# Expert biases of a mixture-of-experts block: loaded as four rows and spread by a VectorE shuffle

## The chip, the cores and the metric

The kernel runs on one core of one Trainium2 chip. The metric is the device time in microseconds (us) of one execution; smaller is better. Three runs of the kernel before took 1596.85, 1597.67 and 1598.76 us.

## What is computed

One residual block over 512 tokens of width 1024 with 16 meta tokens ahead. The first part (a convolution branch, an mLSTM branch and an output projection) isn't touched by the change. The second part is a mixture of experts: a router picks 4 of 32 experts for each token, and each expert computes, for the tokens that chose it,

```
hcat = xb @ w1[e] + b1[e]              # 1024 -> 2048
h_glu, h_lin = split(hcat)             # both clamped at 7.0
act = h_glu * sigmoid(1.702 * h_glu) * (h_lin + 1)
y = act @ w2[e] + b2[e]                # 1024 -> 1024
out = sum over the 4 experts of a token of gate * y
```

All in 32-bit floats. An expert has 8 MB of `w1`, 4 MB of `w2`, 8 KB of `b1` and 4 KB of `b2`.

## The kernel before

The engines each have their own program and meet at semaphores. The first part and the router end with the placing of tokens into slots: each expert has 96 slots (`SLOTS`), cut in three tiles of 32 (`TG = 3`). With the given data one pass over the 32 experts does.

**Weights.** A ring of 12 buffers of 1 MB each holds the weights of an expert: chunks 0 to 7 are `w1` (128 of its rows each), chunks 8 to 11 are `w2`. The SP queue issues all loads in order (`load_block`, `load_chunk`, L484 and L488). Chunk c of expert e is issued when TensorE has used up chunk c of expert e - 1: for c = 0 to 4 one by one through `ring_used`, 5 and 6 the same way at the expert's last tile, 7 with `hid_mm`, and 8 to 11 at the end of the second layer. Behind the last expert's chunks stand the four loads of `y_in`, 2 MB each, which bring back the experts' results in token order for the sums.

**One expert on TensorE (PE).** The hidden layer: for k = 0 to 4 and each tile, four products side by side, one for each group `g` of 32 output partitions (`tile_position=(0, 32 * g)`), of 32 slots by 512 columns (L1619). This layout, in which the 32 partitions of group g hold the 32 slots of a tile and the columns of that group, is why a bias has to stand on 32 partitions at once. After k = 4 come the bias products (below). Then for each tile the k = 5 to 7 (`LATE = 3`), after which the tile is complete (`hid_mm`). The second layer, L1668, follows tile by tile into banks 3 to 5, with the transposes of the next expert's rows (L1606) behind its first tile. Each 32-bit product is two instructions in the trace.

**Biases before.** Ahead of the loop all biases are loaded three times into `bias_rest` (96 partitions of 3 x 1024 values), and VectorE (DVE) subtracts their upper halves (L2077), so that `bias_top` holds three 16-bit parts of each. For each expert, ScalarE (ACT) makes `row_pick`, a matrix that picks that expert's three rows; PE multiplies, four products of 512 columns (L1639) and four of 256 (L1645), into banks 3 and 4; ACT copies them to `bias1` (L1108) and `bias2` (L1110). PE waits for `y_made` ahead of these products, since banks 3 and 4 have held the results of the expert before.

**One expert on the others.** DVE waits for `hid_mm`, adds the bias (L2118), clamps, multiplies, and transposes to `actT` (L2131), tile by tile; then it adds `bias2` to each tile of the second layer as `y_out` (L2144). ACT takes the sigmoid (L1116) and copies the transposed rows to `xT`. GpSimd (POOL) gathers the rows for the expert after next (`xs`, from `u2_rows`) and scatters `y_out` to `y_rows`, both by indirect DMA, through a queue of its own on the same DMA engines.

**Ahead of the loop.** POOL computes `rstd` of each token tile (L610, L611), DVE scales it to `u2` (L1995), and PE, ACT and DVE form logits and choices; POOL writes the token codes to `slot_table` (L717) and reads them back. After the last expert DVE sums: `y_in` times gate (L2187), with the last expert's results added from PE.

## Time and profile before

| | |
|---|---|
| median of three runs | 1597.67 us |
| the profiled execution's own time | 1599.56 us |
| its span, first to last instruction | 1597.8 us |
| outside the span | 1.8 us |
| mean granted clock of TensorE | 0.997 |
| PE busy | 1571.5 us (98%) |
| DVE busy | 649.7 us (41%) |
| POOL busy | 444.7 us (28%) |
| ACT busy | 384.0 us (24%) |
| first hidden product of expert 0 | at 542.06 us |
| moved by DMA | 493.10 MB, of them 384 loads of 1 MB for the ring |

The profile is one execution. Its times are from the start of the span. A matmul's end is modelled and matmuls overlap, so the starts say more than the busy time. In a timeline, a row is a run of like instructions: start, duration, engine, line, operation, output <- inputs, count, and in brackets the idle time ahead of it and what ended it. A landing time is the time from the issue of a transfer to its last part's arrival.

### The profile page before, as it was taken

The numbers are of one execution on the slowest core, as the hardware profiler recorded it, in microseconds if no ns is written. First come the engines' busy times: TensorE is split into PE (matmuls) and PEld (weight loads), VectorE is DVE, ScalarE is ACT, GpSimd is POOL, SyncE is SP. The second block draws the span as 40 slices with busy tenths as digits, with TensorE's granted clock in tenths as the row PEclk, the third lists the DMA queues.
The fourth block names the chain that finished last, engine by engine and source line by source line (L and its number), as shares of the span: only waits on it lengthen the run. The fifth ranks groups of instructions, "written<-read, shape, count | busy, mean of one in ns | idle before, by whom it ended". The sixth has DMA issues, their size and how long they took to land.

```text
span 1597.8 us, 38945 instructions
## 1 busy us (share of the span) xinstructions
PE 1571.5 (98%) x16458; PEld 902.0 (56%) x16458; DVE 649.7 (41%) x1249; ACT 384.0 (24%) x601; POOL 444.7 (28%) x513
## 2 busy tenths in 40 slices
PE   7999999999999999999999999999999999999997
PEld 6998988877889644334433344334433443344334
DVE  4799898016242742224222332233222322232248
ACT  5333134346222311111111121122112111211112
POOL 7334333462433642111211111111211121112114
PEclk9999999999999999999999999999999999999999
DMA  7553242321275699999999999999999999999995
GB/s 217 159 179 112 79 144 95 90 72 51 79 294 224 204 340 406 407 416 414 412 398 410 412 409 398 414 407 408 394 411 407 410 392 404 411 412 400 403 413 236
DMA packets 129781, 493.10 MB, mean 309 GB/s; under 512 B 14379, under 2 KB 72099, under 8 KB 79973
## 3 DMA queue, kind: packets, MB, share of 16 engines
q1 hardware_dynamic: 110932, 464.61, 74.6%
q0 software_dynamic: 9168, 16.78, 3.2%
q10 hardware_dynamic: 9632, 11.03, 2.2%
q8 instruction: 35, 0.57, 0.1%
q14 instruction: 14, 0.11, 0.0%
HBM read 476.32 MB, written 24.87 MB: 314 GB/s over the span
## 4 chain that ended last, share of the span: by engine, by line
PE 95%; POOL 1%; ACT 1%; SPq 1%; DMA 1%; DVE 1%; issue 0%; POOLq 0%; DVEq 0%; ACTq 0%
PE banks L1619 41%; PE banks L1147 27%; PE banks L1668 21%; PE banks L1606 2%; DMA stage<-in_w_in_dram 1%; PE banks L1551 0%; PE banks L1639 0%; SPq L461 0%; PE banks L1506 0%; POOL h_res L787 0%; PE banks L1379 0%; POOL w_lo L624 0%; POOL w_lo L633 0%; POOL small L611 0%; SPq L447 0%
## 5 line engine op out<-in xcount | busy, mean ns | idle before, releaser
L1619 PE MATMUL banks<-w_ring,xT 128*32 128x512 f32 x6144 | 670.9, 592 | 0.1
L1619 PEld LDWEIGHTS banks<-w_ring,xT 128*32 128x32 f32 x6144 | 197.8, 110 | 431.3 <-issue 422.4
L1668 PE MATMUL banks<-w_ring,actT 128*32 128x256 f32 x6144 | 343.9, 380 | 0.0
L1668 PEld LDWEIGHTS banks<-w_ring,actT 128*32 128x32 f32 x6144 | 195.3, 110 | 144.8 <-issue 19.3
L2118 DVE TENSOR_TENSOR hid<-banks,bias 128x512 f32<-128x512 f32 x96 | 63.8, 665 | 475.6 <-PE banks L1619 475.6
L633 POOL TENSOR_TENSOR w_lo<-stage,w_hi 128x2048 fp32r<-128x2048 f32 x38 | 175.3, 4614 | 258.0 <-ACT w_hi L832 258.0
L1147 PE MATMUL banks<-u_hi,w_hi 128*128 128x264 f32 (+1 forms) x528 | 176.8, 335 | 1.5 <-POOL w_lo L624 1.5
L1147 PE MATMUL banks<-u_hi,w_lo 128*128 128x264 f32 (+1 forms) x528 | 175.1, 332 | 0.0
L1147 PE MATMUL banks<-u_lo,w_hi 128*128 128x264 f32 (+1 forms) x528 | 174.7, 331 | 0.0
L706 POOL COPY token_now<-token_of 96x1 int32 x32 | 6.6, 205 | 541.0 <-PE banks L1606 540.9
L1108 ACT ACTIVATE bias<-banks 128x512 f32<-128x512 f32 x32 | 19.1, 598 | 568.4 <-PE banks L1639 568.4
L1809 DVE SCALAR_TENSOR_TENSOR banks<-conv_in,taps,banks 128x512 f32<-128x512 f32 x224 | 151.0, 747 | 0.1
L2144 DVE TENSOR_TENSOR y_out<-banks,bias 128x256 f32<-128x256 f32 x96 | 40.8, 425 | 229.5 <-PE banks L1668 228.3
L1147 PEld LDWEIGHTS banks<-u_hi,w_hi 128*128 128x128 f32 x528 | 99.6, 189 | 11.7 <-POOL w_lo L624 1.7
L1147 PEld LDWEIGHTS banks<-u_lo,w_hi 128*128 128x128 f32 x528 | 99.6, 189 | 10.1
L1147 PEld LDWEIGHTS banks<-u_hi,w_lo 128*128 128x128 f32 x528 | 99.6, 189 | 9.5 <-issue 0.2
L832 ACT ACTIVATE w_hi<-stage 128x2048 fp32r<-128x2048 f32 x40 | 76.4, 1910 | 105.6 <-PE banks L1147 99.0
L695 POOL TENSOR_TENSOR carrier<-carrier 1x1 f32<-1x1 f32 x161 | 33.3, 207 | 240.4 <-DMA y_rows<-y_out,row_now 152.5
L766 POOL DMA_INDIRECT y_rows<-y_out,row_now x93 | 93.5, 1005 | 15.2 <-issue 15.2
L1116 ACT ACTIVATE sig<-hid 128x256 f32<-128x256 f32 x96 | 40.0, 417 | 194.2 <-DVE hid L2119 194.2
L2128 DVE TENSOR_TENSOR act_v<-hid,sig 128x256 f32<-128x256 f32 x96 | 59.8, 623 | 3.5 <-DVE hid L2126 0.3
L1123 ACT ACTIVATE xT<-banks 128x384 f32<-128x384 f32 x64 | 27.9, 488 | 80.0 <-PE banks L1606 80.0
(311 smaller groups left out, 1586.7 us busy)
## 6 DMA issues: line engine op xcount, KB each, us to landing
w_ring<-in_expert_w_dram SPq DMA_DIRECT2D x384, 1024.0 KB, 17.6
stage<-in_w_in_dram SPq DMA_DIRECT2D x20, 1024.0 KB, 5.3
stage<-in_w_in_dram SPq DMA_DIRECT2D x16, 512.0 KB, 5.6
y_rows<-empty_row ACTq DMA_DIRECT2D x8, 1024.0 KB, 4.8
y_in<-y_rows SPq DMA_DIRECT2D x4, 2048.0 KB, 20.8
stage<-in_conv_pw_w_dram SPq DMA_DIRECT2D x4, 1024.0 KB, 5.2
stage<-in_mlstm_out_w_dram SPq DMA_DIRECT2D x4, 1024.0 KB, 5.2
stage<-in_w_out_dram SPq DMA_DIRECT2D x4, 1024.0 KB, 5.5
```

The source lines that it names most:

```text
L633: nc.gpsimd.tensor_tensor(w_lo[:, s], stage[:, s], w_hi[:, s].bitcast(F32), ALU.subtract).then_inc(w_lo_made[s], 1)
L695: nc.gpsimd.tensor_tensor(carrier[:, 1 + i:2 + i], carrier[:, 0:1], carrier[:, 0:1], ALU.add).then_inc(idx_step, 1)
L766: pool.indirect_dma_start(out=y_dram, out_offset=bass.IndirectOffsetOnAxis(ap=row_now[:, t:t + 1], axis=0), in_=y_out[:, t], in_offset=Non ...
L832: nc.scalar.activation(w_hi[:, s], stage[:, s], ACT.Copy).then_inc(w_hi_made[s], 1)
L1116: nc.scalar.activation(sig[:, t], hid[:, t, 0:GRP], ACT.Sigmoid, scale=ALPHA).then_inc(sig_made, 1)
L1147: last = nc.tensor.matmul(dst, l, r, start=(k == 0 and n == 0), stop=(k == KT - 1 and n == 2))
L1619: last = nc.tensor.matmul(banks[32 * g:32 * (g + 1), t].rearrange("p (c j) -> p c j", j=64), xT[:, k, 32 * t:32 * (t + 1)], units, start=k ...
L1668: last = nc.tensor.matmul(banks[32 * g:32 * (g + 1), 3 + t, 0:GRP], actT[:, t, k], w2_ring[k // 2][:, k % 2, GRP * g:GRP * (g + 1)], start ...
L1809: nc.vector.scalar_tensor_tensor(out=to, in0=src, scalar=taps[:, ct, w:w + 1], in1=acc, op0=ALU.mult, op1=ALU.add).then_inc(conv_step, 1)
L2118: own(nc.vector.tensor_tensor(hid[:, t], banks[:, t], bias1.rearrange("p h n -> p (h n)"), ALU.add))
L2128: own(nc.vector.tensor_tensor(act_v[:, t].rearrange("p (c q j) -> p c j q", q=2, j=32), lin.rearrange("p (c j q) -> p c j q", q=2, j=32), ...
L2144: nc.vector.tensor_tensor(y_out[:, t], banks[:, 3 + t, 0:GRP], bias2, ALU.add).then_inc(y_made, 1)
```

## The change

The biases stay in memory and are loaded for each expert as four rows, one for each group g, at partitions 0, 32, 64 and 96 of `bias_row` (zeroed once by POOL; the row for group g holds the 512 hidden and 256 output biases of that group). A VectorE `stream_shuffle` with the mask `[0] * 32` copies the first partition of each 32 over all 32, into `bias`, in 32 bits. The load for the next expert is issued on the SP queue behind its chunk 3, after a wait for the shuffle of the expert before. PE's bias products, ACT's copies and `row_pick`, POOL's `expert_row`, DVE's subtractions, and the threefold load of all biases are gone. PE's wait for `y_made` moves from ahead of the last early products to ahead of the second layer.

```diff
--- before
+++ after
@@ SP, ahead of the loop
-            for m in range(PARTS):
-                sp.dma_start(bias_rest[NE * m:NE * (m + 1), 0:2 * D], expert_b1[0]).then_inc(bias_in, 16)
-                sp.dma_start(bias_rest[NE * m:NE * (m + 1), 2 * D:3 * D], expert_b2[0]).then_inc(bias_in, 16)
+            def load_bias(e):
+                sp.dma_start(bias_row[0:P:32, 0:2 * GRP].rearrange("g (c j) -> g c j", j=64),
+                             expert_b1[0, bass.ds(e, 1)].rearrange("e (c g j) -> (e g) c j", g=CG, j=64)).then_inc(bias_in, 16)
+                sp.dma_start(bias_row[0:P:32, 2 * GRP:3 * GRP],
+                             expert_b2[0, bass.ds(e, 1)].rearrange("e (g n) -> (e g) n", g=CG)).then_inc(bias_in, 16)
+            load_bias(0)
@@ SP, load_block
                     load_chunk(e, c)
+                    if c == 3:
+                        sp.wait_ge(bias_made, n)
+                        load_bias(e)
@@ POOL, ahead of the loop
             pool.wait_ge(mm_done, pair_tick(WO_PAIR + 1, 8))
+            nc.gpsimd.memset(bias_row, 0.0)
...
-            nc.gpsimd.memset(xs, 0.0)
-            for m in range(PARTS):
-                chain(nc.gpsimd.tensor_copy(expert_row[NE * m:NE * (m + 1), 0:NE], ident[NE * m:NE * (m + 1), NE * m:NE * (m + 1)]))
-            nc.gpsimd.tensor_copy(expert_row[:, NE:NE + 1], expert_row[:, 0:1]).then_inc(moe_consts, 1)
+            nc.gpsimd.memset(xs, 0.0).then_inc(moe_consts, 1)
@@ ACT, each expert
-                    act.wait_ge(bias_mm, n * 2 + 1)
-                    nc.scalar.activation(bias1, banks[:, 3].rearrange("p (h n) -> p h n", h=2), ACT.Copy).then_inc(bias_made, 1)
-                    act.wait_ge(bias_mm, n * 2 + 2)
-                    nc.scalar.activation(bias2, banks[:, 4, 0:GRP], ACT.Copy).then_inc(bias_made, 1)
-                    pick_rows(e + 1)
@@ PE, each expert
-                        if k == KT - LATE - 1:
-                            pe.wait_ge(bias_split, PARTS - 1)
-                            pe.wait_ge(y_made, n * TG + 1)
-                            pe.wait_ge(bias_made, n * 3 + 1)
...
-                            for g in range(CG):
-                                last = nc.tensor.matmul(
-                                    banks[32 * g:32 * (g + 1), 3].rearrange("p (c j) -> p c j", j=64), row_pick,
-                                    bias_top[:, 0:2 * D].rearrange("p (c g j) -> p g c j", g=CG, j=64)[:, g],
-                                    start=True, stop=True, tile_position=(0, 32 * g))
-                            last.then_inc(bias_mm, 1)
-                            for g in range(CG):
-                                last = nc.tensor.matmul(banks[32 * g:32 * (g + 1), 4, 0:GRP], row_pick,
-                                                        bias_top[:, 2 * D + GRP * g:2 * D + GRP * (g + 1)],
-                                                        start=True, stop=True, tile_position=(0, 32 * g))
-                            last.then_inc(bias_mm, 1)
@@ PE, second(t)
-                        pe.wait_ge(bias_made, n * 3 + 3)
+                        if t == 0:
+                            pe.wait_ge(y_made, n * TG + 1)
@@ DVE, ahead of the loop
-            dve.wait_ge(bias_in, 16 * 2 * PARTS)
-            for m in range(1, PARTS):
-                rows = slice(0, NE * (PARTS - m))
-                if m > 1:
-                    dve.wait_ge(bias_split, m - 1)
-                nc.vector.tensor_tensor(bias_rest[rows], bias_rest[rows], bias_top[rows], ALU.subtract).then_inc(bias_split, 1)
@@ DVE, each expert (bias1 and bias2 become parts of bias)
-                    dve.wait_ge(bias_made, n * 3 + 2)
+                    dve.wait_ge(y_made, n * TG + 1)
+                    dve.wait_ge(bias_in, n * 32 + 32)
+                    nc.vector.tensor_copy(bias_seen, bias_row[0:1, 0:1])
+                    nc.vector.stream_shuffle(bias, bias_row, [0] * 32).then_inc(bias_made, 1)
+                    dve.wait_ge(bias_made, n + 1)
```

## Rows read from the trace of the kernel before

**Rows 1.** The page: busy us of each engine; DMA busy tenths by slice.

```profile
PE 1571.5 (98%) x16458; PEld 902.0 (56%) x16458; DVE 649.7 (41%) x1249; ACT 384.0 (24%) x601; POOL 444.7 (28%) x513
...
DMA  7553242321275699999999999999999999999995
```

**Rows 2.** Timeline of PE around one expert: start us, us, instruction, count.

```profile
1025.88 13.06 PE L1619 MATMUL banks<-w_ring,xT 128*32 128x512 f32 x120
1038.76 0.41 PE L1639 MATMUL banks<-bias_rest,row_pick 96*32 96x512 bf16 x4
...
1039.11 7.91 PE L1619 MATMUL banks<-w_ring,xT 128*32 128x512 f32 x72
...
1058.13 1.45 PE L1619 MATMUL banks<-w_ring,xT 128*32 128x512 f32 x9
```

**Rows 3.** Ring loads issued from 608 to 1243 us, issue to landing.

```profile
DMA to landing us min/median/max: 12.8/17.6/19.7
```

**Rows 4.** DMA queues, 1012 to 1022 us: packets, MB, share of 16 engines.

```profile
q1 hardware_dynamic: 581, 4.23, 101.6%
```

**Rows 5.** One ring load of a late expert, and its landing.

```profile
L484 SPq DMA_DIRECT2D w_ring<-in_expert_w_dram x1: 333/333/333, 1498.8 to 1498.8; - x1
...
DMA to landing us min/median/max: 22.5/22.5/22.5
```

**Rows 6.** Timeline of PE, 1509.5 to 1536 us.

```profile
1522.90 7.91 PE L1619 MATMUL banks<-w_ring,xT 128*32 128x512 f32 x72
```

**Rows 7.** Timeline of DVE from the last expert on.

```profile
1548.34 1.77 DVE L2177 STREAM_TRANSPOSE selT<-sel_in 128x1536 f32<-128x1536 f32 x1
...
1567.47 3.92 DVE L2187 SCALAR_TENSOR_TENSOR h_res<-y_in,gate_now,h_res 128x1024 f32<-128x1024 f32 x3
...
1574.91 0.42 DVE L2144 TENSOR_TENSOR y_out<-banks,bias 128x256 f32<-128x256 f32 x1 [0.64 <-PE banks L1668]
```

**Rows 8.** Groups by line, DVE: busy us, mean ns, idle before, releaser.

```profile
L2118 DVE TENSOR_TENSOR hid<-banks,bias 128x512 f32<-128x512 f32 x96 | 63.8, 665 | 475.6 <-PE banks L1619 475.6
```

**Rows 9.** DMA queues, 40 to 45 us, while 512 B pieces moved.

```profile
q1 hardware_dynamic: 2064, 1.04, 76.8%
```

**Rows 10.** The page, part 3: the queue of ACT's transfers.

```profile
q10 hardware_dynamic: 9632, 11.03, 2.2%
```

**Rows 11.** DMA issues by line: count, KB each, us to landing.

```profile
y_rows<-empty_row ACTq DMA_DIRECT2D x8, 1024.0 KB, 4.8
...
probs<-head_rows ACTq DMA_DIRECT2D x4, 256.0 KB
inter_bc<-head_rows ACTq DMA_DIRECT2D x4, 256.0 KB, 3.9
...
g_bc<-in_norm_mix_g_dram ACTq DMA_DIRECT2D x1, 512.0 KB, 4.8
...
head_rows<-m_row ACTq DMA_DIRECT2D x1, 8.0 KB
head_rows<-inter_row ACTq DMA_DIRECT2D x1, 8.0 KB
```

**Rows 12.** The first two loads of y_in, issue to landing.

```profile
DMA to landing us min/median/max: 17.1/19.4/21.6
```

**Rows 13.** Timeline ahead of the loop, 526 to 530 us.

```profile
527.55 1.29 DVE L1995 SCALAR_TENSOR_TENSOR u<-h_res,small,gf_bc 128x1024 f32<-128x1024 f32 x1 [1.10 <-POOL small L611]
...
529.04 0.95 POOL L686 MEMSET xs<- 96x1024 f32 x1
...
529.41 0.19 DVE L2015 TENSOR_TENSOR logits<-banks,rb_bc 128x32 f32<-128x32 f32 x1 [0.57 <-PE banks L1569]
```

**Rows 14.** Timeline around the start of the loop.

```profile
541.08 0.96 POOL L717 DMA_INDIRECT slot_table<-code,dest  x1 [0.30 <-issue]
...
542.11 6.72 DVE L2077 TENSOR_TENSOR bias_rest<-bias_rest 64x3072 f32<-64x3072 f32 x2
542.35 3.93 POOL L717 DMA_INDIRECT slot_table<-code,dest  x1 [0.30 <-DVE token_now L2071]
```

24 lines of the change are left out of this document (7 added, 17 removed).

## The prediction, made before the change was run

> **What bounds the kernel now.** I read the page first. TensorE (PE) is busy for 98% of the span, and the busy row of the DMA engines stands at nine tenths in nearly every slice of the second part, at about 410 GB/s [rows 1]. Two resources look full, and a busy share cannot say which one sets the time. So the next view is the timeline of one expert. There PE starts the early products of an expert at 1025.88 us and those of the next at 1058.13: an expert costs 32.25 us, PE never sits idle in it, and the bias products fill the time from the end of a run of 120 products to the start of the next run [rows 2]. PE sets the time, today.
>
> The second question is how far the weights' transfers are from setting it. For that I read the time from issue to landing of the ring's loads. From 608 to 1243 us, some 20 experts, the median stays at 17.6 us and the longest at 19.7 [rows 3]. A transfer that found the engines free would not need that: ten microseconds of pure ring traffic carry 4.23 MB, so 1 MB goes through in 2.48 us, with the queue's packets filling 101.6% of the engines [rows 4]. So about seven loads are always queued. A queue that neither grows nor shrinks over 20 experts is served at just the rate at which it is filled: the engine that lands last needs about 32.25 us for an expert too, and at the end it needs more. In the last experts the load of the eighth chunk, issued at 1498.8, took 22.5 us, against 19.7 before [rows 5], and so landed at 1521.3. PE began the products that need it at 1522.90 [rows 6]. The margin there is 1.6 us. In the middle it was larger: a load issued like it, one period before 1039.11 us [rows 2], was issued at about 1015.0 (1498.8 less 15 periods) and with the longest 19.7 landed 4.4 us ahead.
>
> **What the change takes from PE.** A run of 120 products takes 13.06 us by its row, but its matmuls overlap; starts tell more. From 1025.88 to the first bias product at 1038.76 are 12.88 us, and from there to the next weight product at 1039.11 are 0.35 us [rows 2]. Eight bias products go for each of 32 experts: 32 x 0.35 = 11.2 us. The waits of PE on the bias (`bias_made`, `bias_split`) go as well and cost nothing today, since PE is never idle.
>
> **What it adds on VectorE (DVE).** The shuffle moves 128x768 values. Nearest row: a transpose of 128x1536 in 1.77 us, so half of that, about 0.9 us [rows 7]; it can be no dearer than the whole 1.8 us, which would still be hidden. It stands right after the last `y_out` of the expert before, and DVE then waits for the first `hid_mm`; these waits sum to 475.6 us over 32 experts, some 15 us each [rows 8]. The small copy ahead of it is hidden likewise. In the last expert the selection for the sums stands there too, whose transpose ends at 1550.1, and that expert's late products, whose end DVE waits for, start only at about 1555.2 (1522.90 plus a period) [rows 6, 7]. ScalarE loses three small instructions an expert, off the path. Cost: 0.
>
> **What it adds on SP's queue.** `load_bias(e)` stands behind chunk 3 and waits for the shuffle of the expert before, which is done some 2 us into that expert; chunk 3 is freed at about 10.3 us (four of five runs of 24 products in 12.88 us). Behind the wait stand chunks 4 to 11. It would hold them back only if the bias rows landed over 30 us after their issue (a period of 32.25 less the shuffle and the waits around it). With 20 to 24 us in sight: 0.
>
> **What it adds on the DMA engines.** This is the term that decides. Each expert gets a load of 32 pieces of 256 B (8 KB) and one of 4 pieces of 1 KB, in the same queues as the weights. Price of a piece: while the queue moved 512 B pieces it had 76.8% of 16 engines over 5 us for 2064 packets, 30 ns each [rows 9]. The weights' pieces run at 8192 B in about 310 ns, 26 B per ns [rows 4], so 512 B are 19 ns of bytes and 11 ns of something fixed. Then 256 B are 21 ns, 1 KB is 50 ns; a completion packet is at most the 11. Bounds: bytes alone, 10 and 39 ns; the whole 30 ns for 256 B.
>
> How many engines share it? The trace has transfers of four rows: `head_rows`. The ACT queue moved 9632 packets in all [rows 10]. Its 17 transfers over 128 partitions are y_rows 8 x 1024 packets of 1 KB, probs and inter_bc 8 x 128, g_bc 128: 9344 [rows 11]. The two of four rows are 8 more, which leaves 280 = 17 x 16 + 2 x 4. So a transfer over 128 partitions ends with 16 completions and one of four rows with four: four engines carry it. The bias loads have four rows each. An engine of these four gets 8 x 21 + 50 + 2 x 11 = 240 ns for each expert, 31 times: 7.4 us. By bytes alone it is 8 x 10 + 39 + 22 = 141 ns, 4.4 us; by 30 ns, 312 ns, 9.7 us. Spread over 16 engines, it would be 2 x 21 + 13 + 22 = 77 ns, 2.4 us.
>
> On this the page "DMA: Bandwidth & Descriptors" of the Trainium skill, section "Why a DMA increments its semaphore by 16 and not by 1", says that a transfer runs on the largest number of engines up to 16 that divides the slowest dimension, and on SP's and ACT's queues on the lowest-numbered ones; the count of 280 agrees with the number, and nothing here shows which four. By it, the same four engines would be hit every time; if it failed and 16 shared the load, the sum would be 2.4 us of DMA time in place of 7.4.
>
> **The last stretch.** After the ring come the four `y_in` loads. The first was issued at 1549.42 and landed 17.1 us later, at 1566.5, and DVE's sums over it start at 1567.47: 0.9 us of margin [rows 7, 12]. From there DVE is nearly without a gap to the end; it waited 0.64 us for PE once [rows 7]. So if the transfers end late by x, the end is late by x - 0.9 - 0.6.
>
> **Before the loop.** PE starts the experts at 542. The zeroing of `bias_row` stands on GpSimd (POOL) ahead of the last `rstd`; by the row of 96x1024 in 0.95 us it is 0.7 us. DVE waits for that `rstd` ahead of the last `u2`, which then comes at 528.25 and not 527.55 and ends at 529.5; DVE had 0.57 us idle behind it, and its next step was at 529.41 [rows 13]. Cost: 0.2 us. Against it, the two subtractions of 6.72 us on DVE go; while they ran, an issue of POOL took 3.93 us, where another a little earlier took 0.96 [rows 14]. POOL's table writes then end some 3 to 6 us earlier. They are off PE's path; for the queue it can be worth up to 1.5 us, counted in the range alone.
>
> **Sum.** If nothing but PE bound, -11.2 us. But PE can gain only what the transfers allow: 1.6 us by expert 30, and 0.9 + 0.6 at the tail. The transfers' own chain becomes longer by 4.4 to 7.4 us if one of the four engines is the one that lands last. 4.4 - 1.5 + 0.2 = +3.1; 7.4 - 1.5 + 0.2 = +6.1. The trace does not show which engine lands last, and one outside the four may have a lead that swallows part of it, so I take a value toward the lower of the two: +4.2. On the profiled execution of 1599.56 us this is 1603.8; that execution is 1.9 us above the median of the runs, 1597.67, so the forecast for a median is 1601.9 us.
>
> **Rivals.**
> A. The transfers bind but the bias loads miss the slowest engine, or are spread. Then -1.5 + 0.2, up to +1.1 with 2.4 us of spread load, and -2.8 with the earlier table writes: 1595 to 1599. For it: nothing says which four engines are hit. Against: the first slots of an expert are always filled, so the engines that move the first rows have the most of the gathers too.
> B. PE stays the bound; the flat 17.6 us is a habit of the queue and not a full one. Then -11.2 + 0.2: 1586.7, faster. For it: PE waits for no transfer in the whole loop, and the long landing time could fall when asked to. Against: 101.6% in pure ring traffic [rows 4], and landing times that rose to 22.5 us with PE's period unchanged.
> C. A small transfer holds the queues by itself. A bound is SP's own pace, 0.33 us for an issue [rows 5]; two for each of 31 experts are 20 us of DMA time, 1616. Against: 12 KB in 36 pieces fill no engine for longer than computed. The page "DMA: Bandwidth & Descriptors" of the Trainium skill, section "Bandwidth", gives 0.68 us for a transfer of 4 KB; by it the 62 would hold the queues for 42 us, an estimate.
> D. The wait ahead of `load_bias` holds back chunks 4 to 11. It decides from 30 us of landing time on, and each microsecond above costs one in that expert. Nothing seen is above 23.
>
> **Chances.** Forecast (the four engines count) 0.56, of which a fifth ends under +3.2 us; A 0.27; B 0.12; C and D 0.05. A change of 0.2%, 3.2 us, is about what a measurement of this kernel can tell from none. Slower: 0.56 x 0.8 + 0.05 = 0.50. Faster: B and a little of A's low end, 0.13. Same: 0.37. The likeliest case alone spans +2 to +8.4 (9.7 - 1.5 + 0.2), 1599.7 to 1606.1. With A below it and B, C and D left out (0.17) the range is 1594.8 to 1606.1.
>
> **What would show it.** PE's busy time falls by about 11 us if the products are gone, and PE then has idle time ahead of L1619's later products or of the first products of the second layer, released by the ring's DMA, 14 to 18 us in all, none before about the eighth expert: PE gains 0.35 us and the transfers lose up to 0.24 an expert, against a margin of 4.4 us, used up after some eight experts. The period of late experts stays 32.2 to 32.8 us. Median landing rises to 19 to 23 us. If instead the period is 31.9 to the end, B is right; if late experts are at 33 or more, C. If PE waits for actT early in an expert, the shuffle was not hidden. The forecast is wrong first of all if the engine that lands last is not among those that carry the bias rows.

## The result and the profile after

The changed kernel takes 1602.97 us in the median of 20 runs (1597.35 to 1606.11), the kernel before 1598.46 (20 runs, 1596.85 to 1600.54). The ratio is 1.0025 with a 95% interval of 1.0018 to 1.0031: 4.5 us slower, where 4.2 were forecast. In a later comparison the same kernel had 1.0017 [1.0008, 1.0025] (experiment 6). So it is slower, by a little less or a little more than the 0.2% that was named as the bound of what can be told.

The page, the answer to [rows 1]; the chain of waits by engine; and the costliest group:

```profile
PE 1566.0 (98%) x16202; PEld 914.5 (57%) x16202; DVE 680.3 (42%) x1343; ACT 311.6 (19%) x472; POOL 434.5 (27%) x510
...
DMA  7553243321275599999999999999999999999995
...
PE 69%; DMA 26%; SPq 1%; ACT 1%; POOL 1%; issue 1%; DVE 1%; DVEq 0%; POOLq 0%; ACTq 0%
...
L1608 PE MATMUL banks<-w_ring,xT 128*32 128x512 f32 x6144 | 669.0, 592 | 8.9 <-DMA w_ring<-in_expert_w_dram 8.5
```

The chain and the hidden products on the page of before:

```profile
PE 95%; POOL 1%; ACT 1%; SPq 1%; DMA 1%; DVE 1%; issue 0%; POOLq 0%; DVEq 0%; ACTq 0%
...
L1619 PE MATMUL banks<-w_ring,xT 128*32 128x512 f32 x6144 | 670.9, 592 | 0.1
```

PE issues 256 products fewer and is busy 5.5 us less, and the end is still later. The chain, which was 95% PE, is now 26% DMA. PE waits 8.5 us for the ring ahead of the hidden products; before, its idle time there was 0.1 us. The busy row of the DMA engines has hardly changed, as it was already full.

Landing times of the ring's loads from 608 to 1243 us, against [rows 3]:

```profile
DMA to landing us min/median/max: 12.4/21.0/24.9
```

The timeline of PE, in the middle and in the last experts, against [rows 2, 6]:

```profile
1023.94 21.11 PE L1608 MATMUL banks<-w_ring,xT 128*32 128x512 f32 x192
...
1512.32 13.06 PE L1608 MATMUL banks<-w_ring,xT 128*32 128x512 f32 x120
1526.33 7.93 PE L1608 MATMUL banks<-w_ring,xT 128*32 128x512 f32 x72 [0.96 <-DMA w_ring<-in_expert_w_dram]
...
1545.84 16.52 PE L1608 MATMUL banks<-w_ring,xT 128*32 128x512 f32 x152
```

The bias products between the run of 120 and the run of 72 are gone. Where they stood, PE now waits for chunk 7. From 1512.32 to 1545.84 an expert takes 33.5 us, more than the 32.25 of before (0.3 us of it are two other products of PE ahead of the last expert).

VectorE, groups by line, against [rows 8], with the two new operations (L2101 is the small copy, L2102 the shuffle):

```profile
L2083 DVE TENSOR_TENSOR hid<-banks,bias 128x512 f32<-128x512 f32 x96 | 63.9, 666 | 388.2 <-PE banks L1608 388.2
...
L2102 DVE STREAM_SHUFFLE bias<-bias_row 128x768 f32<-128x768 f32 x32 | 33.0, 1032 | 0.0
L2101 DVE COPY bias_seen<-bias_row 1x1 f32<-1x1 f32 x32 | 4.5, 141 | 61.0 <-DMA bias_row<-in_expert_b_dram 58.6 <-issue 1.2 <-DVE y_out L2111 1.1
```

DVE now waits 58.6 us for the bias rows. That looks like a loss and is none: it still waits another 388.2 us for PE behind it.

The tail: DVE around the first and the fourth sum over `y_in`, against [rows 7], and the landings against [rows 12] (four loads here):

```profile
1570.24 0.42 DVE L2111 TENSOR_TENSOR y_out<-banks,bias 128x256 f32<-128x256 f32 x1 [0.37 <-PE banks L1640]
1571.81 3.96 DVE L2154 SCALAR_TENSOR_TENSOR h_res<-y_in,gate_now,h_res 128x1024 f32<-128x1024 f32 x3 [1.15 <-DMA y_in<-y_rows]
...
1587.13 4.58 DVE L2154 SCALAR_TENSOR_TENSOR h_res<-y_in,gate_now,h_res 128x1024 f32<-128x1024 f32 x2 [0.99 <-DMA y_in<-y_rows]
```

```profile
DMA to landing us min/median/max: 19.2/23.2/25.8
```

Three cuts of the span tell more than its length. They use the first start of a hidden product, the last start of a second-layer product and the end of the span. One line's view of each kernel gives the starts:

```profile
L1619 PE MATMUL banks<-w_ring,xT x6144: 590/592/617, 542.1 to 1562.9; 128*32 128x512 f32 x199
L1668 PE MATMUL banks<-w_ring,actT x6144: 379/379/403, 563.0 to 1574.5; 128*32 128x256 f32 x199
```

```profile
L1608 PE MATMUL banks<-w_ring,xT x6144: 589/592/617, 543.5 to 1566.1; 128*32 128x512 f32 x199
L1640 PE MATMUL banks<-w_ring,actT x6144: 379/379/403, 564.1 to 1577.6; 128*32 128x256 f32 x199
```

The first pair is before, the second after. The loop takes 1574.5 - 542.1 = 1032.4 us before and 1577.6 - 543.5 = 1034.1 after; the tail 1597.8 - 1574.5 = 23.3 and 1602.2 - 1577.6 = 24.6. So the 4.4 us between the two spans are 1.4 ahead of the loop, 1.7 in it and 1.3 behind it. The same cuts for every kernel run here, in the order of the loop's length:

| kernel | bias loads in the loop | start | loop | tail | ratio to before |
|---|---|---|---|---|---|
| half of one chunk left out | as after | 541.0 | 1021.3 | 23.3 | 0.9932 |
| bias loads left out | none | 539.8 | 1027.4 | 24.4 | 0.9972 |
| biases resident | none | 539.5 | 1028.9 | 25.6 | 0.9982 |
| second bias alone | 1 of 4 rows | 540.9 | 1030.6 | 23.8 | 0.9982 |
| before | none (PE products) | 542.1 | 1032.4 | 23.3 | 1 |
| after | 2 of 4 rows | 543.5 | 1034.1 | 24.6 | 1.0025 |
| after, second profile | 2 of 4 rows | 542.4 | 1034.4 | 24.7 | 1.0017 |
| two more DVE copies | 2 of 4 rows | 539.9 | 1034.4 | 24.0 | 1.0019 |
| loads from POOL's queue | 2 of 4 rows | 541.2 | 1035.6 | 25.7 | 1.0031 |
| sixteen-row loads added | 2 of 4, 2 of 16 rows | 541.2 | 1035.6 | 24.1 | 1.0034 |
| doubled | 4 of 4 rows | 542.1 | 1041.4 | 25.1 | 1.0066 |
| doubled, again | 4 of 4 rows | 541.0 | 1040.2 | 24.3 | 1.0078 |

Each row is one profile. The loop of the after kernel repeats within 0.3 us over three profiles (with the two DVE copies), that of the doubled one only within 1.2. The start column moves by 4 us between kernels that do the same work up to there. It is taken up behind the experiments.

### The profile page after: what moved, and what is told of

Same layout as the page of the kernel before. It is cut to its first block, busy times and chain, and to the rows that moved or that the text cites. A ratio compares the mean times of both kernels' runs of the same rounds, so it can differ in the third digit from the quotient of the medians.

```text
span 1602.2 us, 38449 instructions
## 1 busy us (share of the span) xinstructions
PE 1566.0 (98%) x16202; PEld 914.5 (57%) x16202; DVE 680.3 (42%) x1343; ACT 311.6 (19%) x472; POOL 434.5 (27%) x510
## 2 busy tenths in 40 slices
DMA packets 130900, 492.32 MB, mean 307 GB/s; under 512 B 15562, under 2 KB 73410, under 8 KB 81188
## 3 DMA queue, kind: packets, MB, share of 16 engines
q1 hardware_dynamic: 112052, 463.83, 74.1%
## 4 chain that ended last, share of the span: by engine, by line
PE 69%; DMA 26%; SPq 1%; ACT 1%; POOL 1%; issue 1%; DVE 1%; DVEq 0%; POOLq 0%; ACTq 0%
PE banks L1608 28%; PE banks L1136 27%; DMA w_ring<-in_expert_w_dram 24%; PE banks L1640 10%; DMA y_in<-y_rows 1%; PE banks L1595 1%; DMA stage<-in_w_in_dram 1%; PE banks L1540 0%; SPq L457 0%; PE banks L1495 0%; PE banks L1368 0%; POOL w_lo L628 0%; POOL w_lo L637 0%; SPq L443 0%; PE banks L1269 0%
## 5 line engine op out<-in xcount | busy, mean ns | idle before, releaser
L1608 PE MATMUL banks<-w_ring,xT 128*32 128x512 f32 x6144 | 669.0, 592 | 8.9 <-DMA w_ring<-in_expert_w_dram 8.5
L1608 PEld LDWEIGHTS banks<-w_ring,xT 128*32 128x32 f32 x6144 | 207.0, 110 | 451.0 <-issue 445.6
L1640 PEld LDWEIGHTS banks<-w_ring,actT 128*32 128x32 f32 x6144 | 205.3, 110 | 134.8 <-issue 18.0
L2083 DVE TENSOR_TENSOR hid<-banks,bias 128x512 f32<-128x512 f32 x96 | 63.9, 666 | 388.2 <-PE banks L1608 388.2
L768 POOL DMA_INDIRECT y_rows<-y_out,row_now x93 | 93.5, 1006 | 15.1 <-issue 15.1
L2096 DVE STREAM_TRANSPOSE actT<-act_v 128x256 f32<-128x256 f32 x96 | 42.8, 446 | 3.3
```

The lines of the kernel that those rows point to most:

```text
L768: pool.indirect_dma_start(out=y_dram, out_offset=bass.IndirectOffsetOnAxis(ap=row_now[:, t:t + 1], axis=0), in_=y_out[:, t], in_offset=Non ...
L1608: last = nc.tensor.matmul(banks[32 * g:32 * (g + 1), t].rearrange("p (c j) -> p c j", j=64), xT[:, k, 32 * t:32 * (t + 1)], units, start=k ...
L1640: last = nc.tensor.matmul(banks[32 * g:32 * (g + 1), 3 + t, 0:GRP], actT[:, t, k], w2_ring[k // 2][:, k % 2, GRP * g:GRP * (g + 1)], start ...
L2083: own(nc.vector.tensor_tensor(hid[:, t], banks[:, t], bias[:, 0:2 * GRP], ALU.add))
L2096: nc.vector.transpose(actT[:, t].rearrange("p k s -> p (k s)"), act_v[:, t]).then_inc(actT_made, 1)
```

## The experiments

**1. Bias loads left out.** Only the rows of expert 0 are loaded, ahead of the loop; the biases of the other 31 experts are left out of the result.

```diff
                     load_chunk(e, c)
-                    if c == 3:
-                        sp.wait_ge(bias_made, n)
-                        load_bias(e)
...
-                    dve.wait_ge(bias_in, n * 32 + 32)
+                    dve.wait_ge(bias_in, 32)
```

> The changed kernel without the loads of bias rows inside the loop: the rows of expert 0 are loaded once and every expert uses them, so the biases of the other 31 experts are left out of the result. The shuffle stays. Theory (the ring's transfers on the DMA engine that lands last set the time, and the bias loads lengthen them): without them a period of that engine is 32.25 us as before, PE's is 31.9, the margin of 4.4 us (1.6 at the end) is used up late, and PE waits for ring loads only in the last experts, under 9 us in all; the time is 1 to 3 us below the kernel before, ratio 0.998 to 0.9995. Rival 1 (what costs is the shuffle, or the order on SP): the time stays at that of the changed kernel, ratio 1.0025. Rival 2 (PE is the bound once the loads are gone): ratio 0.993.

Measured: 1593.6 us (1592.86 to 1594.68), ratio 0.9972 [0.9961, 0.9982], a larger gain than expected. The line view of the hidden products:

```profile
L1605 PE MATMUL banks<-w_ring,xT x6144: 589/592/617, 539.8 to 1555.7; 128*32 128x512 f32 x199
its engine sat idle before it (us, times) until:
  DMA w_ring<-in_expert_w_dram: 4.0, 9
```

Its timeline at the same two places:

```profile
603.60 20.78 PE L1605 MATMUL banks<-w_ring,xT 128*32 128x512 f32 x192
...
635.51 20.78 PE L1605 MATMUL banks<-w_ring,xT 128*32 128x512 f32 x192
...
1515.97 7.93 PE L1605 MATMUL banks<-w_ring,xT 128*32 128x512 f32 x72 [0.47 <-DMA w_ring<-in_expert_w_dram]
```

The period is 635.51 - 603.60 = 31.91 us, and the chain of waits first runs through the ring at 1199 us. The loop is 6.9 us shorter than in the after kernels (1034.3, the mean of the three with unchanged loads): 0.22 us for each of 31 pairs of loads. It is also 5.0 us shorter than before. So PE's relief is worth 5 us of the loop when nothing is put on the transfers for it. The waits fall to under half of those of after (4.0 against 8.5 us), not to zero: in the last third of the loop the weights alone come too slowly for PE.

**2. Bias loads made twice**, the second time into a spare tile.

```diff
+                sp.dma_start(bias_row2[0:P:32, 0:2 * GRP].rearrange("g (c j) -> g c j", j=64),
+                             expert_b1[0, bass.ds(e, 1)].rearrange("e (c g j) -> (e g) c j", g=CG, j=64)).then_inc(bias_in, 16)
+                sp.dma_start(bias_row2[0:P:32, 2 * GRP:3 * GRP],
+                             expert_b2[0, bass.ds(e, 1)].rearrange("e (g n) -> (e g) n", g=CG)).then_inc(bias_in, 16)
...
-                    dve.wait_ge(bias_in, n * 32 + 32)
+                    dve.wait_ge(bias_in, n * 64 + 64)
```

> The changed kernel with each load of bias rows made twice, the second into a buffer that nothing reads. Theory: the four engines get another 0.21 us for each expert (8 pieces of 256 B, one of 1 KB, two completions), 6.4 us over 31 experts, all of it seen now that PE already waits: ratio 1.0055 to 1.0070, PE's idle time ahead of hidden products from 8.5 to about 15 us. Rival 1 (the loads do not count): ratio 1.0025, idle 8.5. Rival 2 (each small transfer holds the queues for 0.3 us or more): 62 more transfers cost 20 us, ratio 1.015.

Measured: 1609.36 us (1607.47 to 1610.37), ratio 1.0066 [1.005, 1.0081]: 6.4 us above the 1602.97 of the after kernel, inside the expectation. PE waits 15.1 us for the ring ahead of the hidden products. The price of a pair of loads is nearly the same the second time as the first.

**3. The loads issued on POOL's queue.**

```diff
@@ SP
-            load_bias(0)
...
-                    if c == 3:
-                        sp.wait_ge(bias_made, n)
-                        load_bias(e)
@@ POOL (expert 0's two loads stand ahead of the loop)
...
+                def load_bias(e, n):
+
+                    pool.wait_ge(bias_made, n + 1)
+                    nc.gpsimd.tensor_tensor(bias_seen2, carrier[:, 0:1], carrier[:, 0:1], ALU.add)
+                    pool.dma_start(bias_row[0:P:32, 0:2 * GRP].rearrange("g (c j) -> g c j", j=64),
+                                   expert_b1[0, bass.ds(e, 1)].rearrange("e (c g j) -> (e g) c j", g=CG, j=64)).then_inc(bias_in, 16)
+                    pool.dma_start(bias_row[0:P:32, 2 * GRP:3 * GRP],
+                                   expert_b2[0, bass.ds(e, 1)].rearrange("e (g n) -> (e g) n", g=CG)).then_inc(bias_in, 16)
+
                 with pool.Fori(0, NE - 1) as e:
                     n = rows_of_expert(e)
+                    load_bias(e + 1, n)
...
```

> The changed kernel with the same bias loads issued by POOL behind the gather of each expert, on its own queue, and not by SP behind chunk 3. Theory: the bytes still go through the same 16 engines, so the lengthening is gone only if this queue spreads them over other engines than the four which SP's queue uses: then a quarter of 0.21 us for each engine and expert, 1.6 us in all, ratio 1.000 to 1.001; if it uses the same engines, 1.0025. Rival (the place on the SP queue costs, not the bytes): ratio at or under 0.999, since SP then has no wait and no extra issue. POOL's two further issues take some 2 us of the 18 us in which it waits for PE, and cost nothing by either.

Measured: 1603.35 us (1601.86 to 1605.61), ratio 1.0031 [1.002, 1.0042]. This is no better than from SP's queue: the 1.000 to 1.001 of spread loads did not come, and the 1.0025 of the same four engines lies in the interval. PE's timeline of the second expert has part of the reason:

```profile
573.13 20.78 PE L1619 MATMUL banks<-w_ring,xT 128*32 128x512 f32 x192
597.62 5.19 PE L1651 MATMUL banks<-w_ring,actT 128*32 128x256 f32 x64 [3.71 <-issue]
```

This is one new stall, ahead of a second layer, which needs the bias through `actT`: POOL still had its table writes to issue and the tables to read back, and issued the loads of that expert only at 585.15 us, when PE had been in its hidden products for 12 us. Its idle time for the ring over the whole loop is 6.3 us against 8.5, so the ring's part came out somewhat smaller, and the stall gave it back. The two are mixed, and this run settles nothing on which engines POOL's queue uses.

**4. Half of one chunk left out.** The loads stay as in the after kernel, but from expert 1 on only half of an expert's last chunk is fetched; the other half stays that of expert 0, so these rows of `w2` are left out of the result.

```diff
-                    sp.dma_start(w2_ring[m], src).then_inc(ring_in[c], 16)
+                    if m == RING - W1C - 1 and not isinstance(e, int):
+                        sp.dma_start(w2_ring[m][:, 0:1], src[:, 0:1]).then_inc(ring_in[c], 16)
+                    else:
+                        sp.dma_start(w2_ring[m], src).then_inc(ring_in[c], 16)
```

> The changed kernel with the last chunk of the ring half loaded from expert 1 on (512 KB instead of 1 MB, pieces of 4 KB): half of 256 rows of w2 are left out of each expert's load and those of expert 0 are used, so the result is not the reference's. Theory: the transfers get 1.24 us shorter for each expert, so PE never waits for the ring and its period is 31.9 us to the end: 11 us under the kernel before in the loop and up to 1.5 more at the tail, ratio 0.992 to 0.9935. Rival (something else than the transfers holds PE, or the slow end is of another cause): the ratio stays above 0.998.

Measured: 1587.49 us (1586.59 to 1587.65), ratio 0.9932 [0.9916, 0.9947]. Group and timeline:

```profile
L1611 PE MATMUL banks<-w_ring,xT 128*32 128x512 f32 x6144 | 665.1, 592 | 0.1
```

```profile
1466.29 20.78 PE L1611 MATMUL banks<-w_ring,xT 128*32 128x512 f32 x192
...
1498.20 20.78 PE L1611 MATMUL banks<-w_ring,xT 128*32 128x512 f32 x192
```

The period stays 31.91 us to the end, with the bias loads, the shuffle and SP's wait all in place. This is the floor that PE sets: 11.1 us less in the loop than before (1032.4 - 1021.3), the 32 x 0.35 that the prediction read off two gaps. With fewer bytes in the ring, the bias loads cost nothing in the loop. The tail is 23.3 us as before, though the median landing of `y_in` fell from 20.8 to 13.5 us, so the 1.5 us more that were expected there did not come: DVE never waits for `y_in` in either kernel.

**5. The second bias alone in the loop**, so that SP's wait and one of two loads remain. The first bias stays that of expert 0 and is left out for the others.

```diff
+            def load_b2(e):
+
+                sp.dma_start(bias_row[0:P:32, 2 * GRP:3 * GRP],
+                             expert_b2[0, bass.ds(e, 1)].rearrange("e (g n) -> (e g) n", g=CG)).then_inc(bias_in, 16)
...
                     if c == 3:
                         sp.wait_ge(bias_made, n)
-                        load_bias(e)
+                        load_b2(e)
...
```

> In the loop only the second bias (expert_b2, one load of four pieces of 1 KB) is loaded; the first bias stays that of expert 0, so this part of the result is left out. SyncE's wait for the bias ahead of the load is kept. By the price of packets in the queue the load takes about 55 ns of each of four engines, against 208 for both loads. Theory that only the engines' time counts, with the size seen from after to the doubled loads (6.4 us for 208 ns): 4.7 us less than the after kernel, ratio 0.9995. With the size seen from none to after (9.4 us for 31 loads): 6.9 us less, ratio 0.998. Rival that SyncE's wait and issue in the middle of the ring loads costs, whatever is moved: no more than 2 us less than the after kernel, ratio 1.001 to 1.0025, and then the first loads of an expert, not the small ones, are what is late.

Measured: 1594.99 us (1592.98 to 1597.34), ratio 0.9982 [0.9973, 0.9991], 6.0 us under the 1600.96 of the after kernel in the same comparison (experiment 6), of which 3.7 us are in the loop. SP's wait does not cost what the loads do: that rival allowed at most 2 us less than the after kernel. The split is not the one by bytes and pieces: the load of four pieces costs 3.2 us (1030.6 - 1027.4) and the one of 32 pieces 3.7 (1034.3 - 1030.6), where the prices of packets in the expectation give 31 x 55 ns = 1.7 and 4.7. One profile each carries this split, and profiles of one kernel have differed by up to 1.2 us in the loop, so it shows no more than that the small load is not free.

**6. The after kernel again.** No edit.

> The after kernel unchanged, for its ratio to before on the same chip as the others and for a second profile of it: ratio 1.0015 to 1.0035, idle ahead of the hidden products 7 to 11 us. If the drop of TensorE's clock at 383 to 387 us, in work that the change does not touch, belongs to the one execution profiled, it is absent here and the loop starts about 1.4 us earlier; if it comes back, the start of the loop is later again by the same and that part of the loss belongs to the kernel.

Measured: 1600.96 us (1597.07 to 1603.24), ratio 1.0017 [1.0008, 1.0025]; idle ahead of the hidden products 9.3 us, loop 1034.4, tail 24.7. The loop and the tail repeat within 0.3 us. The drop of TensorE's clock of which the expectation speaks was there again, with a start at 542.4.

**7. Two more loads of the same bytes as sixteen rows**, and beside it the kernel of experiment 2 again.

```diff
+                sp.dma_start(bias_row2[0:P:8, 0:128].rearrange("q (k j) -> q k j", j=64),
+                             expert_b1[0, bass.ds(e, 1)].rearrange("e (q k j) -> (e q) k j", q=16, j=64)).then_inc(bias_in, 16)
+                sp.dma_start(bias_row2[0:P:8, 128:192],
+                             expert_b2[0, bass.ds(e, 1)].rearrange("e (q n) -> (e q) n", q=16)).then_inc(bias_in, 16)
...
-                    dve.wait_ge(bias_in, n * 32 + 32)
+                    dve.wait_ge(bias_in, n * 64 + 64)
```

> Beside its own bias loads each expert makes two more of the same bytes, into a spare tile, as sixteen rows (48 pieces of 256 B) where the kernel with doubled loads has them as four rows (32 of 256 B and 4 of 1 KB); nothing is left out. The queue should show 16 completions for each of these loads: 32 x (48 + 32) = 2560 packets more than the after kernel. Theory that the loss is the time of the engines that carry a load (four of them with four rows): here an engine gets three pieces of 18 ns and two completions of 9, 72 ns for each expert, 2.2 us in all, so the loop from the first hidden product to the last second-layer product becomes about 1036.5 us (1034.3 in the after kernel, 1041.35 with doubled four-row loads), ratio 1.003 to 1.0045. Rival that a load costs by itself, whatever engines carry it (its issue, its place in the queues, or its bytes): as the doubled four-row loads, 1041, ratio 1.006 to 1.0075. Rival that completions are dear: between the two or above.

> The kernel with doubled four-row bias loads again, on the same chip as the sixteen-row loads: ratio 1.006 to 1.0075, loop 1041 us by either theory.

Measured: 1604.1 us (1600.84 to 1606.43), ratio 1.0034 [1.0023, 1.0045], and 1610.72 (1607.29 to 1612.0), 1.0078 [1.0064, 1.0092]. The two intervals are apart. Idle ahead of the hidden products, first with sixteen-row, then with four-row loads added:

```profile
L1613 PE MATMUL banks<-w_ring,xT 128*32 128x512 f32 x6144 | 669.3, 593 | 10.1 <-DMA w_ring<-in_expert_w_dram 10.0
```

```profile
L1613 PE MATMUL banks<-w_ring,xT 128*32 128x512 f32 x6144 | 670.0, 593 | 14.0 <-DMA w_ring<-in_expert_w_dram 13.9
```

The same 12 KB for each expert, in the same place of the same queue, lengthen the loop by 1.3 us as sixteen rows (1035.6 - 1034.3) and by 6.5 us as four (the mean of 1041.4 and 1040.2, less 1034.3). This is the experiment that separates most: the bytes, the number of transfers and their place are equal, so none of these makes the loss. What differs is the number of rows, and with it how many engines a load sits on.

SP's issues are not equal, though. Of the added pair they take 0.81 and 0.53 us in the median as sixteen rows, 0.83 and 1.14 as four. And the chain of waits goes through SP's issues (SPq) for 3% of the span in both profiles of the doubled kernel: the issue of a ring load took up to 1.9 us there, where 0.33 is usual, and held back the load behind it. With sixteen-row and with four-row loads added:

```profile
PE 68%; DMA 28%; SPq 1%; ACT 1%; POOL 1%; issue 1%; DVE 0%; DVEq 0%; POOLq 0%; ACTq 0%
```

```profile
PE 58%; DMA 35%; SPq 3%; issue 1%; POOL 1%; ACT 1%; DVE 1%; POOLq 0%; DVEq 0%; ACTq 0%
```

In the after kernel SPq is at 1%, as in before, and gives no sign that its 6.9 us pass through SP. Whether the longer issues of the doubled kernel only follow from a full queue or add to its loss, no run took apart, nor whether the four partitions written matter beside the four engines.

The packets of the queue tell how many engines these are. In order: bias loads left out, after, four-row loads added, sixteen-row loads added, each from its page:

```profile
q1 hardware_dynamic: 110688, 463.45, 74.3%
```

```profile
q1 hardware_dynamic: 112052, 463.83, 74.1%
```

```profile
q1 hardware_dynamic: 113460, 464.22, 74.0%
```

```profile
q1 hardware_dynamic: 114100, 464.23, 74.3%
```

112052 - 110688 = 1364 = 31 x 44, and 113460 - 112052 = 1408 = 32 x 44: 36 data packets and 8 more for two loads, so four completions for each. (The first pair of each kind stands ahead of the loop, 31 are in it.) The sixteen-row pair adds 2048 = 32 x 64. Its first load has 512 B contiguous on both sides, and so goes as 16 pieces and not as the 32 that the expectation counted: the page has 17098 - 15562 = 1536 = 32 x 48 more packets under 512 B, 16 pieces of the second load and 32 completions. That is 16 completions for each load. The page "DMA: Bandwidth & Descriptors" of the Trainium skill, section "Why a DMA increments its semaphore by 16 and not by 1", has a transfer run on the largest number up to 16 that divides the slowest dimension, with one completion for each engine; the packet counts of four kernels agree. That it takes the lowest-numbered ones, no view of these traces shows.

**8. More work on VectorE.** Two copies of all of `bias_row` for each expert, between the wait for the loads and the shuffle.

```diff
+                    nc.vector.tensor_copy(bias_row2, bias_row).then_inc(spare, 1)
+                    dve.wait_ge(spare, 2 * n + 1)
+                    nc.vector.tensor_copy(bias_row2, bias_row).then_inc(spare, 1)
+                    dve.wait_ge(spare, 2 * n + 2)
                     nc.vector.tensor_copy(bias_seen, bias_row[0:1, 0:1])
```

> The after kernel with two more VectorE copies of the whole bias_row (128x768, float to float) for each expert between the wait for the loads and the shuffle, so that the bias comes later by their time, perhaps 0.8 to 2 us for each expert; nothing computed is left out. Theory that VectorE's work on the biases is hidden (it idles 388 us ahead of the additions to the hidden sums): as the after kernel, ratio 1.0015 to 1.0035. Rival that it is on the path: 25 to 60 us more, ratio 1.018 to 1.04.

Measured: 1601.16 us (1598.64 to 1603.89), ratio 1.0019 [1.0009, 1.0029], the loop 1034.4 us. DVE's groups:

```profile
L2085 DVE TENSOR_TENSOR hid<-banks,bias 128x512 f32<-128x512 f32 x96 | 63.9, 665 | 349.8 <-PE banks L1610 349.8
...
L2108 DVE STREAM_SHUFFLE bias<-bias_row 128x768 f32<-128x768 f32 x32 | 32.9, 1027 | 0.0
L2103 DVE COPY bias_row<-bias_row 128x768 f32<-128x768 f32 x32 | 18.0, 562 | 61.5 <-DMA bias_row<-in_expert_b_dram 59.2 <-issue 1.2 <-DVE y_out L2117 1.1
```

Some 1.2 us more for each expert came wholly out of the wait for PE, 388.2 to 349.8 us. The shuffle is hidden.

**9. The biases resident.** All 32 experts' rows are fetched once ahead of the loop, one row for each expert and group, and turned by one block transpose; in the loop SP loads no bias, and DVE widens one column and transposes it back.

```diff
+                for g in range(CG):
+                    sp.dma_start(bias_row[32 * g:32 * (g + 1), 0:2 * GRP].rearrange("e (c j) -> e c j", j=64),
+                                 expert_b1[0].rearrange("e (c g j) -> g e c j", g=CG, j=64)[g]).then_inc(bias_in, 16)
+                    sp.dma_start(bias_row[32 * g:32 * (g + 1), 2 * GRP:3 * GRP],
+                                 expert_b2[0].rearrange("e (g n) -> g e n", g=CG)[g]).then_inc(bias_in, 16)
...
+            chain(nc.vector.transpose(bias_col, bias_row))
...
-                    nc.vector.stream_shuffle(bias, bias_row, [0] * 32).then_inc(bias_made, 1)
+                    nc.vector.tensor_copy(bias_wide.rearrange("p (b j) -> p b j", j=32),
+                                          bias_col.rearrange("p (b e) -> p b e", e=NE)[:, :, bass.ds(e, 1)].to_broadcast([P, 24, 32])).then_inc(bias_wide_made, 1)
+                    dve.wait_ge(bias_wide_made, n + 1)
+                    nc.vector.transpose(bias, bias_wide).then_inc(bias_made, 1)
```

> All experts' biases are fetched once, ahead of the loop, by eight loads into 128 partitions (32 rows for each quarter), and one 32x32 block transpose turns them so that expert e is column e of each block. In the loop VectorE copies that column 32 wide and transposes it back into bias, in place of the seen-copy and the shuffle: the same values on every partition, no bias load and no wait of SyncE in the loop, and no TensorE product. Main theory (the after kernel is late by the bias loads' time on four transfer engines): like the kernel with the loads left out, ratio 0.9965 to 0.998 of before, 1593 to 1595 us; idle ahead of the hidden products under 5 us (8.9 in the after kernel); period of the experts 31.9 us to about the 19th. Rival that VectorE's work on the biases is part of the loss: two operations instead of one and a tiny one, about 1 us more for each expert, so slower than the after kernel, over 1.003. Rival that the gain of the kernel without loads came from not waiting for the bias at all: then nothing is regained here, 1.002 to 1.003.

Measured: 1595.63 us (1592.99 to 1596.77), ratio 0.9982 [0.9973, 0.9991], the full computation. It beats both kernels: 2.4 us under before, 5.3 under the 1600.96 that the after kernel had in the same comparison. The two DVE operations:

```profile
L2101 DVE COPY bias_wide<-bias_col x32: 519/561/564, 546.3 to 1544.3; 128x768 f32 x31, 128x768 f32<-128x768 f32 x1
L2104 DVE STREAM_TRANSPOSE bias<-bias_wide x32: 978/979/981, 546.9 to 1544.9; 128x768 f32<-128x768 f32 x32
```

1.54 us for each expert, hidden like the shuffle. The loop is 3.5 us under before and 1.5 above the kernel without loads. Its tail is the longest but one, 25.6 us. The span of its profile is 3.8 us under that of before: 2.6 us of this are the earlier start, which is not the kernel's own (see below), 3.5 the loop, and the tail gives 2.3 back. DVE waits 2.0 us for `y_in` in it, as in the kernel without loads (1.9 us, tail 24.4); what makes the tail longer still, no run took apart.

**What is left: the start of the loop.** The loops start between 539.5 and 543.5 us. From the last `w_lo` of POOL in the first part (503.66 us before, 505.07 after) to the start of the loop are 38.4 us in all twelve profiles, within 0.1 us. So the difference lies wholly ahead of anything that the change touches, and what it adds and takes away there (the zeroing, the loads, the subtractions) moves the start by nothing that can be seen. In the two profiles of the result the clocks of events agree until 385 us (a step of POOL starts at 384.14 before and 384.12 after), and the like step that follows starts at 392.53 and 393.94: the 1.4 us arise between these. TensorE's granted clock between 340 and 390 us, in the first part of the block, goes with it. Three windows, in order before, after, and the kernel without loads (PE busy, granted clock, DMA share, GB/s):

```profile
340.00:350.00 10.00, 9.82 (x41) 0.93 0.33 107
350.00:360.00 10.00, 10.00 (x43) 0.90 0.09 25
380.00:390.00 10.00, 9.12 (x43) 1.00 0.02 8
```

```profile
340.00:350.00 10.00, 9.82 (x41) 0.90 0.34 107
350.00:360.00 10.00, 10.00 (x44) 0.93 0.11 31
380.00:390.00 10.00, 9.30 (x37) 0.83 0.02 7
```

```profile
340.00:350.00 10.00, 9.82 (x44) 1.00 0.32 107
350.00:360.00 10.00, 10.00 (x46) 1.00 0.18 59
380.00:390.00 10.00, 9.85 (x47) 1.00 0.00 1
```

For some microseconds the clock was at the lower of its two levels, 1.2 instead of 2.4 GHz (0.50 in single microseconds, as at 383 to 385 us in the after kernel, where before has 1.00): twice in the after kernel (0.17 + 0.17 of 10 us there), once in before, never in the third. PE's work ahead of the second drop looks alike in both: 7.37 and 7.33 us busy of the ten from 370 us. The three profiles without a drop (loads left out, resident, more DVE copies) start at 539.5 to 539.9; of the changed kernels the five with one drop start at 540.9 to 541.2 and the three with two at 542.1 to 543.5. Another microsecond of spread is there earlier still: one `w_lo` of POOL starts between 276.55 and 277.86 us. The kernel with two more DVE copies has the after kernel's code up to the loop and no drop, so the drops do not belong to every execution of it. The lists of runs have a mean clock for each. At a mean of 0.998 before has a median of 1597.04 us (19 of 60 runs) and after 1598.40 (9 of 32); at 0.997 it is 1598.59 (37) and 1602.16 (12); at 0.996 or lower there are 4 of 60 runs of before and 11 of 32 of after. (The runs of before come from three comparisons, those of after from two.) The after kernel is slower at each level, but how much of the 4.5 us goes through the clock, and whether the change makes the drops likelier, stays open.

## Why the prediction was right, and where it was not

**The floor of PE.** 32 x 0.35 = 11.2 us, and 11.1 were measured between the loop of before and the one with less to load. PE's own gain is real and is not cashed, so rival B is out: it would have been 1586.7 us, and the half-chunk kernel, where the transfers have room, runs at 1587.49.

**Who lands last.** The forecast let PE gain 1.6 us by expert 30 and took 1.5 into its sum, because the median landing time stayed at 17.6 us for 20 experts and so the slowest engine was taken to need all of the 32.25 us. This step failed. Without bias loads the loop became 5.0 us shorter than before, and loop and tail together 3.9. The landing times of the ring from 608 to 900 us, first before, at a period of 32.25 us, then the kernel without bias loads, at 31.91:

```profile
DMA to landing us min/median/max: 12.9/17.5/19.6
```

```profile
DMA to landing us min/median/max: 12.0/17.3/21.1
```

The median is as flat at the shorter period. A steady landing time says that the transfers keep up; it does not say that they have nothing to spare. What there was to spare was used up over some 20 experts: the longest landing is 21.1 us in this stretch and 24.7 in the next, and the first wait for the ring on the chain belongs to a load issued at 1199 us. From there on the forecast's picture holds: the late experts take 32.5 us each even without bias loads (below), more than the 32.25 of before.

**The price of the loads.** 240 ns for each pair on each of four engines, 7.4 us, with bounds of 4.4 and 9.7. Measured on the loop: 6.9 us for 31 pairs (0.22), 6.5 for 31 more (0.21). The right size, and right in kind, since the sixteen-row pair costs 1.3 us where the estimate for spread loads was 2.4. (The 1.3 is no larger than what two profiles of one kernel have differed by.) So rival A, in which the loads are spread or miss the slowest engine, is out. That the loss is the engines' own time is an inference from the rows and the size; no view shows single engines. That packets set the price inside a pair is not borne out: experiment 5 has the small load at 3.2 us, nearly half, on one profile.

**Loop and tail together.** In the loop -5.0 + 6.9 = +1.9 us. The prediction set 1.5 us of margins against 4.4 to 7.4, had +3.1 and +6.1 as the ends of its sum, and took 4.2 between them. The tail is the other part. The prediction gave it a margin of 0.9 us for the first `y_in` and 0.6 of DVE's slack, and beyond that microsecond for microsecond. DVE did begin to wait for `y_in`, 1.15 us at the first sum and 0.99 at a later one, and the tail grew by 1.3 us (1.1 in the mean of the three profiles with unchanged loads). Where DVE never waits for `y_in`, in before and in the half-chunk kernel, it is 23.3. Loop and tail give +3.0 of the 4.4 us between the two profiles. The other 1.4 lie ahead of the loop, in the clock of a stretch that the change does not touch, which the prediction did not have. The agreement of 4.5 with 4.2 is thus better than the working deserves. The gain was too small by 2.4 us (1.5 for 3.9), the price of the loads too small by 1.4 (5.5 for 6.9), and these partly offset each other; the 1.4 us from elsewhere made up the rest. That the sum came so near is luck.

**Edits costed at nothing.** Right: the shuffle (about 0.9 us forecast, 1.03 measured, hidden); SP's wait (rival D), as experiments 4 and 5 keep it without loss; and ahead of the loop POOL's zeroing of `bias_row`, 0.74 us: the 0.2 forecast for it is not there, as the stretch from 505 us to the start of the loop is as long as before. An issue of POOL at the start of the loop takes 0.96 us, no longer the 3.93 of [rows 14], and the up to 1.5 us held out for it in the range are not seen.

**Rival C**, a small transfer that holds the queues by itself, at 20 us or, by the 0.68 us that the Trainium skill has on the page "DMA: Bandwidth & Descriptors", section "Bandwidth", 42: out. 31 pairs cost 6.9 us, 0.11 us for a transfer. Its other price, SP's pace, was read too low: the issues of the two bias loads take 0.60 and 0.99 us in the median and not 0.33, and still 62 of them cost no more than this.

**What was to be seen.** PE busy 11 us less: 5.5, and 11.5 in the half-chunk kernel (1571.5 - 1560.0), where PE never stalls. Part of a stall is thus booked as busy: the same 6144 hidden products have 669.0 us in the one and 665.1 in the other. Waits for the ring of 14 to 18 us: 8.5 booked, but the loop is 1034.1 - 1021.3 = 12.8 above the floor, so the idle column holds two thirds of a stall; the 12.8 are under the forecast too. None before the eighth expert: the first ring load on the chain is issued at 883.54 us and lands 24.07 us later, in the twelfth. Median landing 19 to 23: 21.0. Late experts at 32.2 to 32.8: up to 33.5, and 33 or more had been named as the sign of C. It is a poor sign. The chain of waits has the late products of the 24th expert, without bias loads and after, at:

```profile
1288.24 7.97 PE banks L1605 x72
```

```profile
1296.40 7.97 PE banks L1608 x72
```

Those of the 31st start at 1515.97 and 1526.33 us, shown above. So of these seven experts one takes (1515.97 - 1288.24) / 7 = 32.5 us without bias loads and 32.8 with them. Most of the slow end is the weights' own.

## What to carry to other kernels

When two resources are full, work taken from one is paid out only down to the other's floor, and what replaces it must not sit on the other. Here 0.35 us of PE for each expert were bought with loads that cost the loop 0.2 us each time, and that sit on four of 16 DMA engines. As far as the runs show, the engine that lands last sets the ring. Small loads in a loop that is full of transfers belong in one fetch ahead of it, or on as many rows as there are engines. To know how much room the transfers have, don't read it from landing times that stay level; take bytes out, or add some, and see when PE begins to wait.

## What the runs showed of the hardware that was not expected

- A pair of loads of 12 KB in a loop costs by its rows: 6.5 us over 31 experts as four rows, 1.3 us as sixteen.
- A load of four pieces of 1 KB costs nearly as much (3.2 us) as one of 32 pieces of 256 B (3.7 us), both on four engines; one profile for each, which leaves the two alike.
- The issue of a four-row load on SP takes 0.54 us at the least and up to 3.2 us in the loop of the after kernel.
- The drop of TensorE's granted clock at 340 to 390 us comes and goes between profiles whose work up to there is the same, and moves all that follows: the starts of the loop lie 4 us apart, as much as the whole effect studied, and in the mean of the changed kernels each drop goes with 1.3 to 1.6 us.
- A DVE copy of 128x768 32-bit values takes 0.56 us, a block transpose of the same 0.98, a shuffle 1.03.
